# A later place for the fp32 group on TensorE, and another order of work on VectorE, in a two-layer encoder with three attention branches

## The reference

```python
h = rms_norm(x, ln_g) * (1.0 + scale) + shift           # shift, scale, gate: silu(c) @ w_ada + b_ada
qa, ka = apply_rope(rms_norm(qa, qn_a)), apply_rope(rms_norm(ka, kn_a))   # A: 4 heads, two maps of 64
ya = rms_norm(softmax(q1 k1) v - lam * softmax(q2 k2) v, subln_a) * (1 - lam_init)
qb, kb = rms_norm(qb, qn_b), rms_norm(kb, kn_b)         # B: 8 heads of 64, neighbourhood 8 x 16 + bias
yb = softmax(qb kb + rpb_b, in the neighbourhood) vb
qc, kc = apply_rope(rms_norm(qc, qn_c)), ...            # C: 4 heads of 128 in 3 groups (window, dilation)
yc = sum over groups of alpha_g * (banded softmax_g) v  # alpha from the softmax denominators
for y_i, z_i, g_i, w_i in the three branches:
    merged += sigmoid(h @ g_i) * ((y_i * silu(h @ z_i)) @ w_i)
x = x + gate * (merged @ w_out)
```

## Time and profile before

| | |
|---|---|
| median of 3 runs | 2547.51 us (2547.23 to 2547.71) |
| the profiled execution | 2546.86 us, its span 2545.1 us |
| PE busy | 2444.3 us (96%) |
| DVE busy | 1409.2 us (55%) |
| ACT busy | 1022.7 us (40%) |
| POOL busy | 92.6 us (4%) |
| mean granted share of TensorE's clock | 0.989 |
| DMA | 171.16 MB, mean 67 GB/s |
| chain that ended last | PE 89%, DVE 4%, ACT 3% |

### The profile page before, as it was taken

How to read it: one execution, slowest core, us unless ns; L and a number is a source line. 1 busy time by engine, 2 the same in 40 slices (tenths; PEclk the granted TensorE clock), 3 DMA queues, 4 the chain that set the end, 5 groups by cost and what they waited for, 6 DMA issues and landing times.

```text
span 2545.1 us, 38346 instructions
## 1 busy us (share of the span) xinstructions
PE 2444.3 (96%) x14514; PEld 2211.4 (87%) x14514; DVE 1409.2 (55%) x4033; ACT 1022.7 (40%) x2720; POOL 92.6 (4%) x141
## 2 busy tenths in 40 slices
PE   2898999999999999999989999999999999999999
PEld 1787888889889999988878788889888999998888
DVE  1876522566437767653468774245753567765432
ACT  2565522454324444341245563145531344444220
POOL 1101000110000000000020100011000000000000
PEclk9899999999999999999989999999999999999999
DMA  6111122111210111131331002211122111112213
GB/s 259 50 52 72 45 72 79 60 57 44 75 65 26 54 50 48 75 115 59 102 108 50 32 18 80 66 53 39 42 73 68 51 51 34 67 61 85 75 59 120
DMA packets 39334, 171.16 MB, mean 67 GB/s; under 512 B 5360, under 2 KB 10096, under 8 KB 37232
## 3 DMA queue, kind: packets, MB, share of 16 engines
q1 hardware_dynamic: 26352, 147.34, 16.8%
q10 hardware_dynamic: 12800, 21.38, 2.5%
HBM read 162.40 MB, written 6.29 MB: 66 GB/s over the span
## 4 chain that ended last, share of the span: by engine, by line
PE 89%; DVE 4%; ACT 3%; ACTq 2%; issue 1%; DMA 1%; SPq 0%; DVEq 0%
PE ps_proj L530 74%; PE ps_pv L643 3%; PE ps_pt L618 3%; PE ps_score L605 2%; PE ps_score L596 2%; PE ps_pv L637 1%; PE ps_tr L658 1%; PE ps_tr L659 1%; ACTq L766 1%; DVE normed L1105 1%; DMA col<-in_cols 1%; DVE top L1188 1%; ACT w_hi L746 1%; DVE act_lo L1096 0%; ACT probs L897 0%
## 5 line engine op out<-in xcount | busy, mean ns | idle before, releaser
L530 PE MATMUL ps_proj<-w_hi,act_hi 128*128 128x384 f32 x1920 | 686.3, 357 | 23.0 <-POOL act_lo L511 14.7
L530 PE MATMUL ps_proj<-w_lo,act_hi 128*128 128x384 f32 x1920 | 663.8, 346 | 0.0
L530 PE MATMUL ps_proj<-w_hi,act_lo 128*128 128x384 f32 x1920 | 663.1, 345 | 0.0
L530 PE MATMUL ps_proj<-act_hi,w_hi 128*128 128x512 f32 (+1 forms) x1408 | 477.4, 339 | 12.1 <-DVE act_lo L1319 6.1
L530 PE MATMUL ps_proj<-act_lo,w_hi 128*128 128x512 f32 (+1 forms) x1408 | 475.2, 338 | 0.0
L530 PE MATMUL ps_proj<-act_hi,w_lo 128*128 128x512 f32 (+1 forms) x1408 | 474.3, 337 | 0.0
L530 PEld LDWEIGHTS ps_proj<-w_hi,act_hi 128*128 128x128 f32 x1920 | 400.3, 208 | 24.8 <-issue 15.7
L530 PEld LDWEIGHTS ps_proj<-w_lo,act_hi 128*128 128x128 f32 x1920 | 401.5, 209 | 0.0
L530 PEld LDWEIGHTS ps_proj<-w_hi,act_lo 128*128 128x128 f32 x1920 | 400.7, 209 | 0.0
L530 PEld LDWEIGHTS ps_proj<-act_hi,w_hi 128*128 128x128 f32 x1408 | 268.1, 190 | 42.6 <-DVE prod L1275 7.3
L530 PEld LDWEIGHTS ps_proj<-act_hi,w_lo 128*128 128x128 f32 x1408 | 267.6, 190 | 28.5
(11 more groups left out here) (142 smaller groups left out, 3165.1 us busy)
## 6 DMA issues: line engine op xcount, KB each, us to landing
w_raw<-in_w SPq DMA_DIRECT2D x128, 768.0 KB, 4.3
w_raw<-in_w SPq DMA_DIRECT2D x40, 512.0 KB, 4.3
w_ada<-in_w_mod SPq DMA_DIRECT2D x11, 1536.0 KB, 6.2
first_ada<-in_w_first SPq DMA_DIRECT2D x4, 2048.0 KB, 14.7
out_y<-merged ACTq DMA_DIRECT2D x16, 384.0 KB, 4.7
merged<-in_x_in ACTq DMA_DIRECT2D x8, 384.0 KB, 28.8
x_old<-in_x_in ACTq DMA_DIRECT2D x8, 384.0 KB, 5.3
x_old<-out_y ACTq DMA_DIRECT2D x8, 384.0 KB, 5.3
```

The lines of the kernel that those rows point to most:

```text
L530: op = pe.matmul(out, sta[s](k), mov[m](k), start=(k == 0 and n == 0), stop=(k == chunks - 1 and n == 2))
```

## The change

A constant `GROUP_AT = 4` is added, and the group on PE stands after chunk index 4, the fifth of the eight, where it stood after chunk index 1, the second. On DVE, `item_end` goes ahead of `tops`, so that the item is done in one piece, and `divisors` goes behind `scale_y` and `low_part`. Two lines are added at the top, so line numbers of the changed kernel are 2 higher.

```diff
+GROUP_AT = 4
...
                 def between(k):
-                    if k == 1:
+                    if k == GROUP_AT:
                         if a0 is not None:
                             scores(a0)
...
                     columns_of(ps_proj, bank, ADA, w_ada[b]).then_inc(*proj_ready.inc(u))
-                    between(1)
+                    between(GROUP_AT)
...
                 if u1 is not None and u1[0] == "b":
                     merge(u1)
+                if u1 is not None and u1[0] == "q":
+                    item_end(u1)
                 if a0 is not None:
                     tops(a0)
-                if u1 is not None and u1[0] == "q":
-                    item_end(u1)
                 if a1 in wide:
                     copy_probs(a1)
-                if a0 is not None:
-                    divisors(a0)
                 if a2 is not None and a2[1] == "A":
                     scale_y(a2)
                 if n - 1 in SPLIT_IN:
                     low_part(SPLIT_IN[n - 1])
+                if a0 is not None:
+                    divisors(a0)
```

## The result

| | median | runs | ratio to before |
|---|---|---|---|
| before | 2547.37 us | 4, 2547.1 to 2547.71 | |
| after | 2650.77 us | 4, 2646.19 to 2652.22 | 1.0403, 95% interval 1.0385 to 1.0421 |

The change makes the kernel 4.0% slower, by 103.4 us; forecast were 59 (2606 us), with 2640 as the upper end of the range. Direction and mechanism came as forecast, the sum was 44 us too small. The profiled run took 2650.95 us, with a span of 2649.2 us and a mean granted clock of 0.977 (before 0.989).

What follows compares the result with a forecast made beforehand. PE bounds the kernel (busy 2444.3 of 2545.1 us) until the loop over ACT and DVE becomes the bound in A. A 40, B 18, C 2 and layer start -1 sum to 59 on 2546.9: 2606 us, range 2568 to 2640.

Steps and rivals of the forecast that it cites:

- The ring in A: A's attention: the loop over ACT and DVE takes 7.83 us per 512-key unit against PE's 7.06; 40 us in all.
- The 5.8 us of slack that the stretch absorbs: A's attention: 5.8 us off 25.8 a layer, for first units without norm of y and unnoticed lateness at the end.
- Part 1: PE's group moves from behind chunk 1 to chunk 4, nine matmuls or 1.6 us later; PE's own work costs 0.
- The wait of qk for the turn: DVE's qk write waits for PE's previous turn (9.4 us before); maxima, exponentials and PE's next scores now stand behind it.
- 2 us to the `a` units and 0 to C: C's attention: loop about 6.5 us against a 7.68 us unit, cost 0; `a` units after it, 2 us (0 to 5).
- For B it said 18 (5 to 28): B's attention: waits behind ACT's eight DMA issues, `a` units following there, and C's items with B's last head; 18 us.
- The forecast keeps 2.4 GHz: Whole kernel: PE's clock stays full, since new waits are 1 to 2 us with full work between; no cost added.
- the granted clock falls in the A stretch: A's attention: one of three signs that would show the forecast wrong; no size given.
- Half absorbed: Rival: handovers are looser than summed, so A costs 22 and B 8; 2576 us, chance 0.11.
- nothing changes: Rival: DVE is busy about half the time, so its order is free; 2547 us, chance 0.05.
- Clock swings: Rival: new waits bring half a unit's matmuls to 1.2 GHz in 36 units, +36 us; 2642 us, chance 0.14.
- The start of a layer: First turn of a layer: its wait for qk goes with the later group; -1 us (0 to -2).

Runs made afterwards that it cites:

- e4: The changed kernel with PE's group back behind the first chunk, leaving both edits on DVE; 2626.31 us, ratio 1.0319 to before.
- r1: The changed kernel with the rope computed on 32 of 256 columns in 36 items of A (heads 1 to 3); 2639.68 us.
- s1: The changed kernel with PE's group behind the first chunk, two qk buffers and ACT's twelve DMA issues dealt out over A's heads 1 and 2; 2591.08 us.
- r6: The kernel before with ACT's twelve DMA issues dealt out and two buffers for qk; 2529.50 us, ratio 0.9936.
- r5: The changed kernel with ACT's twelve DMA issues dealt out over the units of A's heads 1 and 2; 2634.81 us.
- r2: The changed kernel with two buffers for qk, so qk no longer waits for the turn of the item before; 2618.57 us.
- e1: The kernel before with only PE's group moved behind the fourth chunk, DVE's order unchanged; 2560.71 us, ratio 1.0062.
- r4: The changed kernel with PE's group back behind the first chunk in z, g, b and o units only; 2639.78 us.
- r3: The kernel before with ACT's twelve DMA issues dealt out, one per unit of A's heads 1 and 2; 2528.74 us, ratio 0.9928.

## Why the prediction was right in kind and wrong in size

- **The ring in A: right.** Its period is 8.05 us (7.83 forecast), the head 50.1 us (49.0), and e4, r1 and s1 show that it is DVE's order and DVE's time that set it. That the head came so close is in part luck, since its parts were less well sized than their sum: the unit behind a head's change is short (6.53 us), the narrow unit with a low part alone takes 10.8 instead of 8.3 (9.7 at full clock, in s1).
- **The 5.8 us of slack that the stretch absorbs: failed.** That is the term "I take off 5.8 for what the stretch absorbs", which left 20 a layer (its two reasons, 2 x 1.25 and some 3, make 5.5). Measured are 26.6 in layer 1: 6.6, 9.65 and 10.3 us in the three heads. Only the first head absorbs, 2 us; at the end nothing is given back. The clock can account for 3.4 of the 26.6, so for half of what lies above the 20. In s1 the same layer loses 29.2 against r6, with at most 1.7 of clock and, by r5, about 1.5 from the issues. In layer 0 the three heads lose 26.9, of which up to 10.2 can be clock; how much of the rest is missing slack stays open there. A is 13.5 us of the 44. The 4.7 beside B's first items, where the forecast had nothing, are another matter: with two buffers for qk they are gone (0.2 in r2, 0.1 in s1) while A's loss stays, so they belong to the wait of qk.
- **Part 1, "PE's own work stays the same, cost 0": failed.** The wait lay in a stretch of which I had only said that the `b` units have no group. The first two z units of each branch have one, and the chain from the last turn over ACT's table load and sigmoid to PE's bank already ended behind PE: the waits of before hold an entry of 6.0 us in six places that I had passed over, `ps_proj` for `prod`. So nine matmuls more in front of the turn could only be paid in full. 11.7 us were lost there, 6 x 1.07 in the wait, 3 x 1.6 in the clock behind it and 0.5 in two first z units; e1 shows it with no other edit, and r4 takes it away.
- **The wait of qk for the turn: seen, priced too low at the end of a layer and in C.** The forecast named maxima, exponentials, and PE's next scores as what stands behind qk, and then gave 2 us to the `a` units and 0 to C, where 11.9 were lost. r2 gives them all back. For B it said 18 (5 to 28), measured 22.5, and named the places rightly: behind eight DMA issues PE's unit loses 1.7 to 2.8 us in three of the four heads, and the `a` units with the unit behind them 3.0 and 5.4. The reason was half right: in r2 the three lose nothing, so it is again the wait of qk ahead of the maxima.
- **"The forecast keeps 2.4 GHz": failed in part.** The mean clock fell from 0.989 to 0.977; over the span, 2545.1 x 0.011 = 28 us of full speed were missing before and 2649.2 x 0.023 = 61 after. The 33 us between them are a ceiling, since much of the slow time falls into units that would wait for the loop anyway; the table has them by stretch. The prediction's own sign of being wrong, that the granted clock falls in the A stretch, came true. Over the three heads of layer 0 it is 0.92, before 0.97; in layer 1, the second and the third head (before 1.00 and, for the wait for y_t, 0.93):

```profile
1452.00:1503.00 51.00, 44.58 (x253) 37.17 (x252) 34.41 (x100) 27.00 (x92) 0.00 (x0) 0.97 0.09 32
...
1503.00:1563.00 60.00, 45.59 (x248) 38.23 (x247) 35.69 (x99) 27.12 (x92) 7.28 (x12) 0.91 0.10 34
```

  The loop does not need it (1.00 in s1's head of 51.3 us, 0.97 in after's of 50.1), but it can be up to 13.7 of A's 53.5. That the clock can fall behind a single wait of about 2 us is plain in the z units: the same 1.07 us of added wait costs 1.07 in three places and 2.7 in the three others. The rule of the Trainium skill, "TensorE: Matmul & The Clock Gate", section "A second HAM failure mode: psum-queue depth-cycling", that frequent short idle times make the clock swing, is borne out in part: over 65 us of s1's A stretch PE waits in every unit and the clock holds at 1.00, in after it falls for a few us at a time, to 0.92 over the three heads of layer 0.
- **The rivals.** "Half absorbed" (2576) and "nothing changes" are refuted by the head of 50.1 us. "Clock swings" named 2642 us and so came nearest, partly by luck. It put 36 us into A, where the clock can explain 13.7 at most, and s1 shows the loop's loss with no swing; but of the 44 us beyond the forecast the clock can be up to 33, and no run tells it apart from the late group and the wait of qk, with which it goes (r2, r4 and s1 are missing 46, 48 and 24 us of full speed against 62 in after). The start of a layer gave no gain that a run can tell from noise (-2.8 to +2.8 us over the kernels, also in those that leave it alone).

## What to carry to other kernels

When an order on a side engine changes, write the loop of both helper engines with its waits and compare its length with the main engine's unit; if it comes out longer, take off nothing for slack that no row shows: two of the three heads here lost the whole excess and more. Then walk through every kind of unit that the moved block touches, also those in which it is nearly empty, and look there for waits that the main engine already has: what ends them has no room at all. A turn that stands nine matmuls later cost 11.7 us in six such places here. And a wait put ahead of a step whose result the main engine needs in the same unit wants a second buffer: 32 us of 103 were that wait.

## What the runs showed of the hardware that I had not expected

- One DMA issue of 0.59 to 0.7 us on ACT's queue runs beside the operation that ACT has just started, so single issues between operations cost ACT nearly nothing. Twelve in a row stopped ACT for 8.4 us and cost PE 8.5 to 8.75 us a layer; dealt out, in r3, they cost nothing (in r5, 1.5 us in one head of four).
- The switch of ACT to the sigmoid takes a table load of 1.28 us. In all six z places, before and after, it starts 0.02 us behind ACT's copy and 2.67 us ahead of the matmul for which PE waits, so PE waited behind it in the kernel before too, only less (6.0 us in all against 12.5).
- Behind which of the six waits in the z units (1.7 to 2.5 us each) the clock falls differs from kernel to kernel: A of both layers and B of layer 0 in after, A of layer 0 and C of both layers in e1, with the same order of work on PE.
